# Transposed inverse blocks by VectorE's 32x32 transposes in a hybrid RWKV-7 / S5 step

## The reference

```
def step(S, inp):
    r_t, w_t, k_t, v_t, ma_t, b_t = inp
    sa = jnp.einsum('dbhij,dbhj->dbhi', S, ma_t)
    S = S * w_t[..., None, :] + sa[..., None] * b_t[..., None, :] + v_t[..., None] * k_t[..., None, :]
    return S, jnp.einsum('dbhij,dbhj->dbhi', S, r_t)
```

## Time and profile before

| | |
|---|---|
| median of 3 runs | 2572.7 us (2570.61 to 2576.2) |
| the profiled execution: time, span | 2570.66 us, 2568.7 us |
| TensorE busy, of the whole span | 2093.2 us (81%), 21540 products |
| VectorE busy | 1239.2 us (48%), 2498 instructions |
| ScalarE busy | 758.3 us (30%) |
| GpSimd busy | 649.7 us (25%) |
| mean granted TensorE clock | 0.892 of full speed |

### The profile page before, as it was taken

The page is one execution under the profiler, slowest core; times in us unless marked ns, Lnnn a source line. Parts: engine busy times, 40 slices in busy tenths (PEclk is TensorE's granted clock), DMA queues, the critical chain, the costliest instruction groups (busy, mean ns, idle before and its releaser), DMA issues. The chain is left out here.

```text
span 2568.7 us, 50592 instructions
## 1 busy us (share of the span) xinstructions
PE 2093.2 (81%) x21540; PEld 1373.1 (53%) x21540; DVE 1239.2 (48%) x2498; ACT 758.3 (30%) x1682; POOL 649.7 (25%) x720
## 2 busy tenths in 40 slices
PE   7673445475649899988898989769999999999998
PEld 2342334233436787677677778634555455455453
DVE  1469999730153545464546454434333333323325
ACT  2302223311123434343434444323322122112111
POOL 1407552212111212222222222113221211211253
PEclk9676777787769999999998999879999999999999
DMA  7200000441100000000000000052211011011112
GB/s 280 76 1 5 10 10 11 142 162 58 29 9 12 14 3 11 10 17 11 2 10 5 3 3 7 2 208 91 91 66 66 1 66 66 18 49 66 50 38 94
DMA packets 62691, 120.25 MB, mean 47 GB/s; under 512 B 5946, under 2 KB 25402, under 8 KB 61682
## 3 DMA queue, kind: packets, MB, share of 16 engines
q1 hardware_dynamic: 62468, 117.02, 12.9%
HBM read 97.56 MB, written 17.35 MB: 45 GB/s over the span
## 5 line engine op out<-in xcount | busy, mean ns | idle before, releaser
L83 PE MATMUL psum<-arena 128*128 128x384 bf16 (+3 forms) x2244 | 739.1, 335 | 125.1 <-ACT arena L1700 27.9
L84 PE MATMUL psum<-arena 128*128 128x384 bf16 (+3 forms) x2244 | 738.4, 335 | 0.0
L85 PE MATMUL psum<-arena 128*128 128x384 bf16 (+3 forms) x2244 | 737.6, 335 | 0.0
L1652 ACT ACTIVATE arena<-psum 128x256 f32<-128x256 f32 (+5 forms) x900 | 289.8, 333 | 529.1 <-PE psum L1524 141.4
L83 PEld LDWEIGHTS psum<-arena 128*128 128x128 bf16 (+1 forms) x2244 | 224.3, 100 | 311.5 <-issue 78.7
L85 PEld LDWEIGHTS psum<-arena 128*128 128x128 bf16 (+1 forms) x2244 | 224.9, 100 | 172.1 <-issue 9.7
L84 PEld LDWEIGHTS psum<-arena 128*128 128x128 bf16 (+1 forms) x2244 | 224.4, 100 | 164.1 <-issue 7.5
L2637 DVE TENSOR_TENSOR arena<-arena 128x384 f32<-128x384 f32 x96 | 106.9, 1113 | 234.7 <-ACT arena L2513 234.7
L1524 PE MATMUL psum<-arena 64*64 64x64 f32 x2880 | 179.7, 222 | 10.7 <-DVE arena L2201 10.7
L2652 DVE TENSOR_TENSOR arena<-arena,psum 128x512 f32<-128x512 f32 x108 | 74.2, 687 | 196.7 <-PE psum L85 196.7
L1524 PEld LDWEIGHTS psum<-arena 64*64 64x64 f32 x2880 | 159.4, 137 | 15.0 <-DVE arena L2201 14.8
(11 more groups left out here) (298 smaller groups left out, 3251.3 us busy)
## 6 DMA issues: line engine op xcount, KB each, us to landing
arena<-in_w_ff SPq DMA_DIRECT2D x16, 2048.0 KB, 8.5
arena<-in_w_ada SPq DMA_DIRECT2D x12, 2048.0 KB, 8.3
x<-arena SPq DMA_DIRECT2D x18, 512.0 KB, 2.8
arena<-x SPq DMA_DIRECT2D x18, 512.0 KB, 3.2
arena<-in_w_in SPq DMA_DIRECT2D x12, 512.0 KB, 4.0
arena<-in_x SPq DMA_DIRECT2D x9, 512.0 KB, 8.9
out_y<-arena SPq DMA_DIRECT2D x9, 512.0 KB, 2.7
arena<-in_w_out SPq DMA_DIRECT2D x2, 2048.0 KB, 10.6
```

Source lines behind the costliest of these rows:

```text
L83: nc.tensor.matmul(out, whi, xhi, start=first, stop=False)
L84: nc.tensor.matmul(out, wlo, xhi, start=False, stop=False)
L85: return nc.tensor.matmul(out, whi, xlo, start=False, stop=last)
L1652: copy = lambda out, src: nc.scalar.activation(out, src, ACT.Copy)
```

## The change

The starting products and ScalarE's copy of them (`begin` on TensorE, `begun`) go. VectorE's new `begin` transposes `xt0` straight into `xx[..., 0]`, right behind the last state update of the step before. At levels 1 to 4 `merge_x` makes half 0 alone, and ScalarE copies that half alone. VectorE's new `flip` makes half 1 of level l-1 from half 0 by transposes, at the head of `merged` for level l, that is, ahead of its reset and its predicated copies. VectorE's transpose works on each 32x32 block by itself; up to level 4 the inverse is zero outside its diagonal blocks of 32, so that the transpose of the blocks is that of the whole. Level 5 is as before. TensorE's waits move along: `merge_q` of level 1 waits for VectorE (`x0`), `merge_x` also for `flipped`, and the wait for `x_last` stands at level 5 (before: at the start).

```
             def local(i):
                 ct = unit(2 * i)[0]
+                pe.wait_ge(ev("masked"), 2 * i + 2)
...
             def merge_q(i, l):
                 for q in H2:
-                    pe.wait_ge(ev("x0_read", q) if l == 1 else ev("inv", l - 1, q), i + 1)
+                    pe.wait_ge(ev("x0", q) if l == 1 else ev("inv", l - 1, q), i + 1)
...
                 for q in H2:
                     pe.wait_ge(ev("q_read", l, q), i + 1)
+                    if l > 1:
+                        pe.wait_ge(ev("flipped", l - 1, q), i + 1)
+                    if l == NLEV - 1:
+                        need(pe, ev("x_last", q), i)
...
                             if l < NLEV - 1:
-                                mm(xblock(b, q, h, 0), xt, grow[b, l - 1, q, h], start=True, stop=True)
-                            last = mm(xblock(b, q, h, 1), grow[b, l - 1, q, h], xt, start=True, stop=True)
+                                last = mm(xblock(b, q, h, 0), xt, grow[b, l - 1, q, h], start=True, stop=True)
+                            else:
+                                last = mm(xblock(b, q, h, 1), grow[b, l - 1, q, h], xt, start=True, stop=True)
...
 (ScalarE's merged)
                     if l < NLEV - 1:
-                        copy(xx[:, q].rearrange("p h n c -> p (h n c)"), LANE[q][:, 0:2 * P]).then_inc(ev("inv", l, q), 1)
+                        copy(xx[:, q, :, 0], src[:, :, 0]).then_inc(ev("inv", l, q), 1)
...
 (VectorE)
+            def begin(i):
+                for q in H2:
+                    dve.wait_ge(ev("xt0"), 4 * i + 2 * q + 2)
+                    nc.vector.transpose(xx[:, q, :, 0], xt0[:, q]).then_inc(ev("x0", q), 1)
+
+            def flip(i, l):
+                for q in H2:
+                    dve.wait_ge(ev("inv", l, q), i + 1)
+                    nc.vector.transpose(xx[:, q, :, 1], xx[:, q, :, 0]).then_inc(ev("flipped", l, q), 1)
+
             def merged(i, l):
+                if l > 1:
+                    flip(i, l - 1)
                 reset(i, l)
...
                 if i > 1:
                     advanced(g - 1)
+                if inv:
+                    begin(i)
                 side.until(at)
```

More of the change, by code:

```diff
@@ L1578, in body @@
                     leave(g - 1)
-                if inv:
-                    begin(i, 0)
-                    begin(i, 1)
                 side.until(at)
@@ L1784, in beside @@
                         yield from entry(z, ENTRY[1, 1], c, 1, 1)
[L1786 to L1790, removed]
             def local(i):
@@ L1801, in merged @@
                     act.wait_ge(ev("xq", l, q), i + 1)
+                    src = LANE[q][:, 0:2 * P].rearrange("p (h n c) -> p h n c", h=2, n=2)
                     if l < NLEV - 1:
-                        copy(xx[:, q].rearrange("p h n c -> p (h n c)"), LANE[q][:, 0:2 * P]).then_inc(ev("inv", l, q), 1)
+                        copy(xx[:, q, :, 0], src[:, :, 0]).then_inc(ev("inv", l, q), 1)
                     else:
-                        copy(xf[i % 2][:, q], LANE[q][:, 0:2 * P].rearrange("p (h n c) -> p h n c", h=2, n=2)[:, :, 1])\
-                            .then_inc(ev("x_last", q), 1)
+                        copy(xf[i % 2][:, q], src[:, :, 1]).then_inc(ev("x_last", q), 1)
             def turned_out(i):
@@ L1835, in body @@
                     out(g - 1)
-                if inv:
-                    begun(i)
                 side.until(at)
```

## The result

The changed kernel takes 2581.8 us (median of 20 runs), the kernel before 2572.2 (median of 20): the ratio is 1.0043, with a 95% interval from 1.0033 to 1.0053. It is slower, where I forecast 2538 and faster. Its runs lie between 2574.4 and 2596.2 us, those of before between 2568.2 and 2576.2. The profiled run, 2590.6 us with a span of 2588.8, is one of its longer ones.

The account below looks back on a forecast made before the run. TensorE's own work was taken to bound most steps, VectorE's queue parts of others; 94 us of products removed less 27, 7, 4, 6, 4, 3 and 9 left 34 us saved, forecast 2538 us, range 2512 to 2572.

Parts of the forecast that it names:

- The clock: TensorE idles more at levels 4 and 5; 30 us more at 1.2 GHz, costing 9 us.
- Rival B: The clock gives the saving back: a quarter of the stage at 1.2 GHz, about 2574 us; chance 0.10.
- The start: VectorE's starting pair behind the state's update: no saving in about 12 steps (6 us), side work pushed back (4 us).
- the plain step's forecast of 16.0: A step without side work goes from 17.56 to about 16.0 us: three of five savings stay.
- the products removed: Five groups of 16 instructions at 0.52 us in 36 steps leave TensorE: 94 us saved.
- the transposes' cost: 360 transposes added on VectorE at about 300 ns, 0.50 us for a pair.
- rival A: The fp32 transpose on VectorE is dear; with a pair of 1.5 us, slower at 2625 us; chance 0.10.
- levels 4 and 5: The pair between mask and predicated copies lengthens TensorE's wait in 53 places by 0.50 us: 27 us given back.
- level 2: VectorE idles 0.79 us before the copies in a plain step, so the pair fits in there.
- rival C: VectorE's chain is the real bound: all 180 pairs show, 90 us against 94, no change, 2569 us; chance 0.09.

Follow-up runs that it names:

- e2: The changed kernel with the transposes for levels 4 and 5 moved ahead of the masks on VectorE: 2563.4 us, 0.9976 of before.
- e3: The changed kernel with the start undone (starting products on TensorE and ScalarE's copy back), the transposes of levels 1 to 4 kept: 2570.3 us, 1.0006 of before.
- e5: e4 with 16 instructions of products nobody reads at the old place of the starting products: 2574.5 us, 1.0012 of before.
- e1: The changed kernel with products nobody reads at the starting products' old place and ahead of levels 4 and 5's growth products: 2568.8 us, 0.9983 of before.
- e10: The changed kernel with products nobody reads in place of all five groups that it removed from TensorE: 2604.7 us, 1.0127 of before.
- e7: e6 with 16 instructions of products nobody reads behind the last solution of a step: 2556.8 us, 0.9947 of before.
- e4: The kernel before with the start alone moved to VectorE, all other transposed halves left on TensorE: 2587.2 us, 1.0063 of before.
- e6: The changed kernel with the edits of e2 and e3 together: 2548.4 us, 0.9911 of before.
- e8: e6 with the mask of unit 2i+2 behind level 4's predicated copies in place of ahead of them: 2559.8 us, 0.9950 of before.

## Why the prediction was wrong

**The step that failed is "The clock".** I put a third more half-speed time, 30 us, and 9 us of loss for it. The profiles have 170 us more, and the medians of the runs 161. The price was not wrong: I took 0.6 x 0.5 = 0.30 us for each, and the changed kernel's own runs have 0.32, those of e2 and e3 0.27 and 0.29. So the loss is 161 x 0.27 to 0.32, that is 43 to 51 us, and not 9. Without its clock term my sum has 43 us saved; the measured loss of 9.6 us and 43 to 51 us for the clock leave 34 to 42. The sum's other terms, taken together, were thus about right, and the amount of half-speed time turned a gain into a loss. That time and clock go together in the runs of one kernel is no proof of a cause; e5 is one, by an edit that leaves VectorE alone, for the start, and e1 gives back part of the whole change's loss by the same means.

I sized the term by the plain step's 1.00 at the gaps of the kernel before. The change takes products away besides making the gaps longer, and e10 points to the load as the greater part. Rival B had the mechanism and the price, and the sign that I named for it came (a clock under 0.9 in the stage); its amount, 120 us more, was too small and its chance of 0.10 too low. Its number is wrong as well: 2574 counts the forecast's 9 us twice, and 120 x 0.30 comes to 2565.

The section of the Trainium skill that I set beside it (TensorE: Matmul & The Clock Gate, A second HAM failure mode: psum-queue depth-cycling) tells of a loss through brief idling between groups of products. The traces agree in part: 0.95 against 0.86 with 82 against 125 us of idle time in the changed kernel, but in e7 0.90 with 83.

**"The start" was wrong too.** I let its 0.52 us count in some two thirds of the steps, 9 us in all after its other terms, since I looked for what waits on VectorE, and not for what else the entering product waits for. Its second condition, ScalarE's copy of y, came 0.45 us later than the end of the products before it and had been hidden by the very products that went (e4: 17.55 for 17.56). With that, the plain step's forecast of 16.0 becomes 16.5, as e1 and e3 have it. By the runs of e4 the start saves 1 to 4 us at an unchanged clock (63 us at 0.27 to 0.32, less the 16 lost).

**Right were:** the products removed; the transposes' cost (285 to 290 ns, a pair 0.49 to 0.50 for 0.50 forecast), which ends rival A; levels 4 and 5, where the pair behind the mask gives back most of what the level before saved (waits of 0.56 and 0.66 for 0.15 and 0.28, so 0.4 of 0.52, and 22 us over the stage for 27); and level 2, where it is hidden. Without the start (e3) the terms add up to 34 us at an unchanged clock, and the runs have 0.9 saved and 110 us at 0.29 to 0.32, that is 33 to 36. Plain steps of 17 us and more, the sign of rival C, did come (17.88 and 19.88), but at clocks of 0.88 and 0.76. C falls by the steps at full clock (16.57 for 17.77) and by e6, where with the pairs moved 1.9 us of the plain step's 17.56 are saved.

**Open:** what in TensorE's activity decides the clock. Less work came with a lower one (e4), filler with a higher one in e1, e5 and e10 and with a lower one in e7. With shorter waits alone it hardly rose in e2, and in e8 it fell. Nor do the runs show why the clock of one kernel differs from run to run, by 68 us of half-speed time between the lowest and the highest of the changed kernel's runs.

## What to carry to other kernels

Work that is taken off TensorE can cost clock: here 34 to 42 us saved came with 161 to 170 us more at 1.2 GHz, and that took 43 to 51 back. Price a removal at both levels of the clock, and look at the granted clock of the stage after. Before counting a removed group as saved, read every condition of the instruction behind it; the group may have been the cover of a wait that no list of waits shows yet. And where an engine's queue has an idle stretch, put the new work there: the transposes of levels 1 to 4, with two of the four pairs ahead of the masks and the start left on TensorE (e6), turned 0.4% slower into 0.9% faster.

## What the runs showed of the hardware that I had not expected

Products whose results nothing reads made a kernel faster: 2587.2 to 2574.5 us (1.0063 to 1.0012 of before), with 88 us at 1.2 GHz in place of 147. In the changed kernel the granted clock fell to 0.76 in a plain step of 285 products, while another of its steps, with 288, kept 1.00 at waits of 0.56 and 0.66 us. And 20 runs of this one kernel had mean granted clocks from 0.854 to 0.866 and took 2596.2 to 2574.4 us.
